# Index layer of a two-block transformer on one core: new column order, top-k rounds beside later columns, memory products between attention steps

## The reference

```python
def even_mixer(x, w_in, ckv_gain, w_uk, w_uv, sinks, w_out, rel_table):
    q_a, c_kv, q_i, k_i, w_i, q_b, k_b, v_b = split_cols(x @ w_in, EVEN_WIDTHS)   # 512,128,512,64,8,512,128,128
    o_a = dsa_attention(...)      # index scores pick 64 keys per query, attention over latents
    o_b = banded_attention(...)   # causal window of 128 keys, sinks
    return concatenate([o_a, o_b]) @ w_out

# in dsa_attention, per block of 128 queries
    act = relu(einsum('bqhd,bsd->bqhs', qi_b, k_i) * IDX_DIM ** -0.5)
    score = einsum('bqh,bqhs->bqs', wi_b, act)
    score = where(kpos <= qpos, score, -1e30);  sel = top_k(score, 64)

# in cross_attention
    k = mem @ w_k;  v = mem @ w_v
```

## Time and profile before

| | us |
|---|---|
| Median of 3 runs | 2604.91 (2604.16 to 2604.93) |
| Profiled execution | 2608.45 |
| Its span | 2606.7 |
| PE busy | 2524.2 (97%) |
| DVE, ACT, POOL busy | 1991.7, 1163.7, 74.9 |
| The changed stretch, 990.95 to 1126.70 | 135.75 |

### The profile page before, as it was taken

One profiled execution on the slowest core, in us unless ns is written; L12 is line 12 of the kernel. 1 busy time (PEld: TensorE's weight loads), 2 busy tenths in 40 slices (PEclk: granted clock), 3 DMA queues, 4 the chain that ended last, 5 costly groups with the idle time before them and its releaser, 6 DMA issues.

```text
span 2606.7 us, 42896 instructions
## 1 busy us (share of the span) xinstructions
PE 2524.2 (97%) x16960; PEld 2157.3 (83%) x16960; DVE 1991.7 (76%) x2450; ACT 1163.7 (45%) x1487; POOL 74.9 (3%) x104
## 2 busy tenths in 40 slices
PE   8999999999999999889999989999999999999998
PEld 5877888888879999678999787888888888888886
DVE  4958777778647885647888747888888888889887
ACT  4354100003311002442003646777777777777776
POOL 0100100000000000000001100000000000000000
PEclk9999999999999999999999999999999999999999
DMA  8714544443225544123554222999899989999996
GB/s 343 286 74 162 186 169 169 168 168 123 81 101 220 185 177 146 65 98 114 181 189 153 109 98 109 374 362 374 336 375 362 375 336 371 368 352 358 363 374 247
DMA packets 90393, 599.66 MB, mean 230 GB/s; under 512 B 9728, under 2 KB 12800, under 8 KB 23552
## 3 DMA queue, kind: packets, MB, share of 16 engines
q1 hardware_dynamic: 77280, 543.20, 55.2%
q0 software_dynamic: 12960, 54.26, 5.8%
HBM read 596.37 MB, written 1.05 MB: 229 GB/s over the span
## 4 chain that ended last, share of the span: by engine, by line
PE 91%; DVE 4%; ACT 2%; DMA 1%; issue 1%; SPq 0%; DVEq 0%; ACTq 0%
PE bank L1108 13%; PE bank L1111 13%; PE bank L1112 13%; PE bank L2275 8%; PE bank L2279 8%; PE bank L2278 8%; PE bank L2306 4%; PE bank L2310 4%; PE bank L2309 4%; PE bank L503 3%; DMA ring<-in_stream 1%; PE bank L1376 1%; ACT arena L1398 1%; PE bank L519 1%; PE bank L1355 1%; PE bank L543 1%
## 5 line engine op out<-in xcount | busy, mean ns | idle before, releaser
L928 DVE TENSOR_TENSOR ring_part<-ring,arena_part 128x2048 fp32r<-128x2048 f32 (+1 forms) x480 | 1077.8, 2275 | 28.5 <-ACT arena_part L2598 12.4
L2598 ACT ACTIVATE arena_part<-ring 128x2048 fp32r<-128x2048 f32 x339 | 647.5, 1920 | 196.4 <-DMA ring<-in_stream 195.3
L1108 PE MATMUL bank<-arena_part 128*128 128x256 f32 (+1 forms) x2184 | 699.5, 320 | 19.4 <-DVE h_part L928 6.4
L1112 PE MATMUL bank<-arena_part,ring_part 128*128 128x256 f32 (+1 forms) x2184 | 695.0, 318 | 0.0
L1111 PE MATMUL bank<-h_part,arena_part 128*128 128x256 f32 (+1 forms) x1656 | 526.4, 318 | 0.0
L1108 PEld LDWEIGHTS bank<-arena_part 128*128 128x128 f32 x2184 | 418.5, 192 | 57.5 <-issue 25.0
L1112 PEld LDWEIGHTS bank<-arena_part,ring_part 128*128 128x128 f32 x2184 | 418.6, 192 | 27.5
L2275 PE MATMUL bank<-arena_part,h_part 128*128 128x512 f32 x896 | 354.1, 395 | 0.0
L2279 PE MATMUL bank<-arena_part,h_part 128*128 128x512 f32 x896 | 349.6, 390 | 0.0
L2278 PE MATMUL bank<-ring_part,h_part 128*128 128x512 f32 x896 | 348.9, 389 | 0.0
L1111 PEld LDWEIGHTS bank<-h_part,arena_part 128*128 128x128 f32 x1656 | 317.3, 192 | 20.1
(11 more groups left out here) (350 smaller groups left out, 2867.6 us busy)
## 6 DMA issues: line engine op xcount, KB each, us to landing
ring<-in_stream SPq DMA_DIRECT2D x515, 1024.0 KB, 4.9
arena<-in_ada_stream POOLq DMA_DIRECT2D x80, 512.0 KB, 4.5
consts<-in_small POOLq DMA_DIRECT2D x1, 2800.0 KB, 11.5
arena<-in_c_rows POOLq DMA_DIRECT2D x2, 1024.0 KB, 6.1
arena<-in_ab_bias POOLq DMA_DIRECT2D x1, 2048.0 KB, 9.9
arena<-in_t_bias POOLq DMA_DIRECT2D x1, 2048.0 KB, 9.2
x_stream<-in_x_t SPq DMA_DIRECT2D x1, 1024.0 KB, 7.4
x_stream<-in_ctx_t SPq DMA_DIRECT2D x1, 1024.0 KB, 9.2
```

Source lines behind the costliest of these rows:

```text
L928: return nc.vector.tensor_tensor(low, value, high.bitcast(F32), ALU.subtract)
L1108: m = nc.tensor.matmul(out_ap, w_high, high, start=start, stop=False)
L1112: return nc.tensor.matmul(out_ap, w_low, high, start=False, stop=stop)
L2598: nc.scalar.activation(high, ring[:, where], ACT.Copy).then_inc(sem("moe_high"), 1)
```

## The change

The columns now come in the order q_i, k_i, c, q_a, q_b, k_b, v_b. PE makes six columns, the head weights and the sum of c's squares, and then lays index scores between the four q_a columns: four heads behind each. The slots are split by other engines: ACT rounds slots 2 to 7 and the first two of the output projection (`ev_rounded`, `slot_high_act`), DVE makes the low part of slot 2, POOL those of all others (`pool_low`), in one queue with the two masks. Three areas in turn hold the high parts. On DVE each add of a head of the second block of queries is followed by a top-k round of the first block; k_b and v_b are copied out behind the last round. The memory products are cut into pieces of four (`mem_group`) and put in front of certain steps of the two attentions on PE, in a bank of their own (7); the attention outputs share bank 6. ACT copies a group out at the steps of `DSA_DONE` and `BAND_DONE`. The latents and their squares move to another place. On the host, the columns of the weights are reordered.

```diff
-        ev_slot_high = next_slot_high(1, 8)
+        EV_AT = FFN_AT[1] + SLOTS_FFN
+        ev_areas = [part_area(8192, SLOT)] + [slot_high[(EV_AT + i) % 2] for i in range(2)]
+        ev_slot_high = {EV_AT + n: ev_areas[n % 3] for n in range(8)}
         OD_AT = FFN_AT[2] + SLOTS_FFN
...
+        cT = area(17616, 256)
         q_iT = area(1280, 1024, "p (c t) -> p c t", c=4)
...
+        EV_ATT_OUT, MEM_BANK = 6, 7
+        DSA_UNITS = {("T", a): (a // 2, 4) for a in range(6)}
+        DSA_DONE = {("S", 4): 0, ("V", 2): 1, ("V", 4): 2}
+        BAND_UNITS = {("T", 0): (4, 4), ("T", 1): (4, 4), ("V", 0): (5, 4), ("T", 2): (5, 4)}
+        BAND_DONE = {("V", 0): 4, ("V", 2): 5}
...
-            split_products(bk, w, 15, next_high, h_part, SEQ, ev_slot_high)
...
+            marks["ev_split"] = bk.count["slot_split"]
...
+            def ev_columns(n):
+                more_split_products(bk, w, n, next_high, h_part, SEQ, ev_slot_high)
+
+            def index_scores(t, heads):
+                for h in heads:
+                    b = bk.next_bank()
+                    pe.wait_ge(free(b), bk.emptied())
+                    r, c = half(h % 2), h // 2
+                    nc.tensor.matmul(PS[b][:, X2], q_iT[r, c, t * P:(t + 1) * P], k_iT[r, :], start=True, stop=True)\
+                        .then_inc(full(b), 1)
+
+            split_products(bk, w, 4, next_high, h_part, SEQ, ev_slot_high)
+            ev_columns(2)
+            index_taken = bk.all_freed(bk.turn - 6, 5)
             small_token_products("w_idx", 8)
             sum_pe(bk, "c_squared", lambda c: c_sq, SEQ, 1)
+            lat_from = []
+
+            def latent_query():
+                ev_columns(1)
+                lat_from.append(bk.freed(bk.turn - 1))
+
+            latent_query()
+            for taken in index_taken:
+                pe.wait_ge(*taken)
+            index_scores(0, range(4))
             rstd_pe(bk, SEQ)
-            pe.wait_ge(*bk.freed(bk.turn - 1))
+            c_normed = bk.freed(bk.turn - 1)
+            latent_query()
+            index_scores(0, range(4, 8))
+            pe.wait_ge(*c_normed)
             b = bk.next_bank()
             pe.wait_ge(free(b), bk.emptied())
             for t in range(2):
                 m = nc.tensor.transpose(PS[b][:, t * P:(t + 1) * P], cT[:, t * P:(t + 1) * P], ident)
             m.then_inc(full(b), 1)
+            c_tok_taken = bk.freed(bk.turn - 1)
+            for at in (0, 4):
+                latent_query()
+                index_scores(1, range(at, at + 4))
+            ev_columns(4)
+            band_from = [bk.freed(bk.turn - n) for n in (4, 3, 2, 1)]
+            ev_columns(1)
+            b = bk.next_bank()
+            pe.wait_ge(free(b), bk.emptied())
+            tiles = [w.tiles()[0] for _ in range(DC)]
+            for t in range(2):
+                for k in range(DC):
+                    m = nc.tensor.matmul(PS[b][:, t * P:(t + 1) * P], xv[:, k, t * P:(t + 1) * P], tiles[k],
+                                         start=k == 0, stop=k == DC - 1)
+            m.then_inc(full(b), 1)
+            band_from += [bk.freed(bk.turn - n) for n in (2, 1)]
             uk = small_at("w_uk", "p (c n) -> p c n", c=4)
-            for taken in bk.all_freed(bk.turn - 19, 16):
+            for taken in lat_from:
...
-            for taken in bk.all_freed(bk.turn - 24, 8):
+            for taken in bk.all_freed(bk.turn - 8, 8) + [c_tok_taken]:
                 pe.wait_ge(*taken)
-            mem_products()
+            mem_parts, mem_done = [], []
+
+            def mem_group(group, n):
+                begun = mem_done.count(group)
+                if begun == 0:
+                    pe.wait_ge(free(bk.fill(MEM_BANK)), bk.emptied())
+                    if group == 4:
+                        mem_parts.extend(w.slots(2))
+                for k in range(begun, begun + n):
+                    mem_done.append(group)
+                    if group < 4:
+                        tile, first = w.tiles()
+                        m = nc.tensor.matmul(PS[MEM_BANK][:, X2], tile, xv[:, k, SEQ:TT], start=k == 0, stop=k == DC - 1)
+                    else:
+                        t, half_at = group - 4, k // 4
+                        part = mem_parts[half_at][:, k % 4 * 512:(k % 4 + 1) * 512]
+                        m = nc.tensor.matmul(PS[MEM_BANK][:, :], xv[:, k, SEQ + t * P:SEQ + (t + 1) * P], part,
+                                             start=k == 0, stop=k == DC - 1)
+                        first = k % 4 == 0 and t == half_at
+                    if first:
+                        m.then_inc(sem("slots_used"), 1)
+                if begun + n == DC:
+                    m.then_inc(full(MEM_BANK), 1)
+
+            def mem_beside(units):
+                def beside(what, a):
+                    if (what, a) in units:
+                        mem_group(*units[what, a])
+                return beside
+
             pe.wait_ge(sem("bias_landed"), 48)
-            outs = attention_pe(bk, dsa_steps())
+            outs = attention_pe(bk, dsa_steps(), mem_beside(DSA_UNITS))
+            mem_group(3, DC)
...
+            for taken in band_from:
+                pe.wait_ge(*taken)
+            attention_pe(bk, band_steps(), mem_beside(BAND_UNITS))
 
...
+            def ev_rounded(n, begun=None):
+                slot_high_act(bk, EV_AT + n, ev_slot_high, fresh=begun is None, used=None if begun is None else EV_AT + begun + 1)
+
+            def index_relu(t, heads):
+                for h in heads:
+                    n = 8 * t + h
+                    if n >= 2:
+                        act.wait_ge(sem("score_added"), n - 1)
+                    to(relu_buf[n % 2], ACT.Relu, cols=SEQ, scale=64 ** -0.5)
+
+            ev_rounded(2)
             for c in range(4):
                 to(q_iT[:, c, :], cols=SEQ)
+                if c == 1:
+                    ev_rounded(3, begun=1)
+            ev_rounded(4, begun=2)
+            bk.turn += 2
+            sqrt_table()
+            act.wait_ge(*bk.freed(bk.turn - 1))
+            nc.scalar.activation(c_sq, cT, ACT.Square).then_inc(sem("c_squared"), 1)
             bk.turn += 1
+            root_act(bk, SEQ, 1, n=P)
+            to(q_aT[:, 0, :], cols=SEQ)
+            ev_rounded(5, begun=3)
+            index_relu(0, range(4))
+            bk.turn += 1
+            to(q_aT[:, 1, :], cols=SEQ)
+            index_relu(0, range(4, 8))
+            to(c_tok[:, :, :].rearrange("p t e -> p (t e)"), cols=SEQ)
+            for c in (2, 3):
+                to(q_aT[:, c, :], cols=SEQ)
+                if c == 2:
+                    ev_rounded(6, begun=4)
+                index_relu(1, range(4 * c - 8, 4 * c - 4))
             for c in range(4):
                 to(q_bT[:, c, :], cols=SEQ, scale=64 ** -0.5)
...
+                if c == 0:
+                    ev_rounded(7, begun=5)
...
+            slot_high_act(bk, EV_OUT, ev_out_high, fresh=True)
+
+            def mem_out(group):
+                b = bk.fill(MEM_BANK)
+                act.wait_ge(full(b), bk.filled())
+                if group < 4:
+                    ins = nc.scalar.activation(mem_keys[0][:, group, :], PS[b][:, X2], ACT.Copy)
+                else:
...
+            attention_act(bk, dsa_steps(), mem_beside(DSA_DONE))
+            mem_out(3)
...
+            slot_high_act(bk, EV_OUT + 1, ev_out_high, fresh=True)
+            attention_act(bk, band_steps(), mem_beside(BAND_DONE))
...
-            def split_ev(n, cols=SLOT):
-                at = FFN_AT[1] + SLOTS_FFN + n
-                split_slot(bk, at, None, used=at if n > 2 else None, highs=ev_slot_high, cols=cols)
+            slot_low_dve(bk, EV_AT + 2, ev_slot_high)
+            marks["ev_rounded"] = bk.count["slot_rounded"]
+            bk.up("slot_rounded", 7)
...
+            def add_index(t, h):
+                dve.wait_ge(*bk.freed(bk.turn))
+                bk.turn += 1
+                wi, s = w_heads[:, t, h:h + 1], idx_score[:, t, :]
+                rb = relu_buf[h % 2]
+                if h == 0:
+                    ins = nc.vector.tensor_scalar(s, rb, wi, None, ALU.mult)
+                else:
+                    ins = nc.vector.scalar_tensor_tensor(s, rb, wi, s, ALU.mult, ALU.add)
+                ins.then_inc(sem("score_added"), 1)
+                dve.wait_ge(sem("score_added"), bk.up("score_added"))
+
+            def top_round(t, r):
+                if r == 0:
+                    dve.wait_ge(sem("score_masked"), t + 1)
+                s, wk = idx_score[:, t, :], idx_work[:, t, :]
+                src = s if r == 0 else wk
+                nc.vector.max(top8[:, t, :], src).then_inc(sem("dve_step"), 1)
+                dve.wait_ge(sem("dve_step"), bk.up("dve_step"))
+                nc.vector.match_replace(wk, top8[:, t, :], src, -3e38).then_inc(sem("dve_step"), 1)
+                dve.wait_ge(sem("dve_step"), bk.up("dve_step"))
+
+            def top_mask(t):
```

(64 more changed lines are left out.)

121 lines of the change are left out of this document (27 added, 94 removed).

## The result

The changed kernel takes **2615.07 us** (median of 5 runs, 2613.68 to 2621.89) where the kernel before took 2604.93 beside it: a ratio of 1.0036, 95% interval 1.0026 to 1.0047. It is slower by 0.4%, outside the range of the prediction (2595 to 2612). In a second comparison, with 7 runs against 29 of before, the ratio was 1.0033 (1.0022 to 1.0044). That settles the size: some 9 us.

The account below looks back on a forecast made before the run. PE, busy 97% of the span, was taken as the bound. Columns and index lose 5.2 us, memory in the attention gains 9.6, net -4.4; DVE held by POOL adds 7.3, so +2.9 on 2604.9 gives 2607.8 us, range 2595 to 2612.

Parts of the forecast that it names:

- The wait for slot 6: Index layer's columns: PE waits for POOL's low part, queued behind its second mask; 8.4 us, 9.4 with DVE held.
- The exclusion: DVE work reading only SBUF is held while POOL forms a low part; 7.3 us in sum.
- the mask add: Second sparse step: DVE's add waits for output slot 0's low part on POOL, first turn 4.1 us later.
- the band's scaling: Band attention: DVE's first scaling waits for output slot 1's low part on POOL, 1.5 us.
- The 2.0 us of clock behind the sparse step's first turn: Sparse attention: PE's clock is low after the hole ahead of the first turn, 2.0 us.
- Rivals 1, 2 and 4: No exclusion for tensor-tensor forms (2600.5, 0.24); POOL's queue not late (2590.9, 0.14); memory groups delay PE's turns (2610.5, 0.08).
- The attention with memory in it and nothing held: Sparse scores to output projection, memory groups between turns: 62.2 us against the old 71.8, gain 9.6.
- later waits: Attention steps: waits after the held DVE instructions shrink by 1.3 us, as softmax and turns are then ahead.
- The charge of 2.0 us for the clock behind slot 6's wait: Index layer: PE's clock is low after the new stall, as after an earlier hole; 2.0 us charged.
- the account of part 1: Columns and index: some 6 us gained, less 8.4 stall, 2.0 clock and q_lat copies; 5.2 us lost.
- rival 3: Head-weight product: clock drops, dense columns follow at half clock, 2.4 us lost; 2610.2 or more, chance 0.12.
- a difference of spans carries over: Whole kernel: the span's change was added unchanged to the median time, 2604.9 + 2.9 us.

Follow-up runs that it names:

- low6_first: The changed kernel with POOL forming the low part of slot 6 ahead of the second mask instead of behind it; median 2608.1 us.
- adds_first: The changed kernel with all eight score adds of the second 128 tokens ahead of the first block's top-k rounds on DVE; median 2609.0 us.
- out_lows_dve: The changed kernel with the low parts of the first two output slots made by DVE behind the sparse step, not by POOL; index layer 133.50 us.
- adds_and_out_dve: The changed kernel with score adds ahead of top-k rounds and the first two output slots' low parts on DVE; median 2598.8 us, ratio 0.9975 to before.
- columns_alone: The changed kernel with memory products in one block ahead of the sparse attention again and two output banks in both attention steps; median 2620.1 us.
- memory_alone: The kernel before with only the change's memory groups between the turns of the two attention steps; median 2621.2 us.

## Why the prediction was wrong, point by point

**The steps that held.** The wait for slot 6 was forecast at 8.4 us, or 9.4 with the exclusion, because POOL's second mask comes about 1037: it was 8.7 us, and the mask came at 1039.49. The exclusion between DVE and POOL was taken from one scalar instruction on 16 columns and spread to all DVE work in SBUF: it held for tensor-tensor forms too, in the mask add (3.84 over its own 0.42, forecast 4.1), the band's scaling (2.24, forecast 1.5) and, in low6_first, an add (3.72). The max and replace rounds weren't held (0.43 and 0.41 us in adds_first beside the low part at 1032.23, as elsewhere), and they were covered, as forecast. The 2.0 us of clock behind the sparse step's first turn was 2.0. The sparse scores were forecast 70.1 us behind the first column (1060.1 + 1.0, from 990.95) and came after 70.7 in the first profile. From there to the output projection 68 to 70 us were forecast and 68.8 to 69.1 measured. Rivals 1, 2 and 4 are out.

**The sizes that were off inside it.** The attention with memory in it and nothing held was walked to 62.2 us; in out_lows_dve and adds_and_out_dve, which also have ACT's rounding off the chain, it took 60.7. The 1.1 us of half clock in that walk never came there: the two rows of out_lows_dve have clock 1.00. The 0.6 us between its sum of 62.8 and the 62.2 stands in no run. So the memory products between the turns are worth up to 71.8 - 60.7 = 11.1 us, not 9.6. Against that, the band's hold and the rounding cost 2.3 us together, where the sum had 1.5 and took 1.3 off for later waits. These nearly cancel.

**Readings that were wrong and did no harm.** The charge of 2.0 us for the clock behind slot 6's wait was 1.9, 2.2 and 2.4 in the three profiles, but the reading under it was wrong. Ahead of 978.07 there was no hole of 12 us in before:

```profile
978.07 0.36 PE L1108 MATMUL bank<-arena_part 128*128 128x256 f32 x1 [1.75 <-DVE ring_part L928]
```

It was 1.75 us, and the clock was at half speed for 3.4 us behind it (5 x 0.34 / 0.5), not for nearly 5; that the charge came out is luck. And the account of part 1 (6 gained, less 8.4 and 2.0 and 2.9 of copies) gives -7.3 us, not the -5.2 of the walk; the forecast used the walk.

**The step that failed** is rival 3's chance and its size: "the clock drops in the head-weight product", 0.12, 2.4 us. The sum put this term at nothing. The trace of before had shown the clock at 0.50 from 1042 on the earlier trace rows, behind the same piece of 8-column products. I read that as a drop *in* a stretch of small work, which dense columns around it would prevent. The dense columns didn't prevent it; they came to run at half speed. It happened in two of the three profiles of the change, at 1.7 and 3.4 us, and put the index layer at 141.4 and 143.3. With the 1.7 us that the same two lose at the output projection it is a mean of (1.95 + 3.77 + 2 x 1.7) / 3 = 3.0 us (0.3 of it the longer half speed behind slot 6), about half of what was missing. The chain was right, and the clock under it wasn't. Rival 3 had named the mechanism, at 2.4 us; its 2610.2 or more is still under the measured time.

A second step failed beside it: "a difference of spans carries over". It put the time outside the span at no change, and that grew by 1.4 us.

**The frame.** The forecast took 2604.9 as the base; the larger sample says 2606.5. That would have moved the forecast up to 2609.4, still some 6 us short of 2615.1 to 2615.8.

**The sum.** The mean index layer of the three profiles of after is 141.4 us, 5.7 over before. The rest of the span is 2471.0 in the mean of three against 2470.5 in two: +0.6, with the drop at the output projection in it. Outside the span (time less span) before spends 1.80 us, between 1.74 and 1.84 in all its runs; the change spends 2.1 to 3.6, 3.2 in the median: +1.4. Together 7.7. The median spans of all runs differ by a little more, 2612.6 - 2604.7 = 7.9, as the two profiled executions of before were 1.5 us over its median; 7.9 + 1.4 = 9.3 is the difference of the medians. Against the forecast's 2.9 that leaves 6.4 us: 2.8 in the index layer, 0.6 in the rest of the span, 1.4 outside it, and 1.6 that the profiles show less than the medians. Of the 2.8, the first profile, without a drop, has 0.8: 0.5 ahead of the sparse scores and 0.3 behind.

**What stays open.** What the 1.4 us outside the span are: columns_alone and memory_alone have 1.97 and 1.96, all others derived from the change 2.3 to 3.4 in the median, and no view shows that time. Why the clock also drops at the output projection in two of three profiles of the change. And where the profiled executions of before lost 1.5 us to its median.

## What to carry to other kernels

Read an engine's queue for what stands behind each wait: here a 0.4 us mask, put behind the eighth add, kept a weight slot from PE for 8.7 us, and moving only DVE's adds gave 6.8 us back. A low part on POOL is not free for DVE: place it where DVE works out of PSUM or not at all, and check whom a held instruction feeds, down to the bank that a copy behind it frees. And when a change moves a piece of small products from among other small work to between dense ones, price the clock behind it into the sum and take more than one profile: an execution with no drop looked like a forecast come true.

## What the runs showed of the hardware that I had not expected

- The clock fell while PE had no idle time in the profile: behind 32 products of 8 columns (3.5 us) PE was 100% busy and its mean clock was 0.66 over 5 us, or 0.57 over 8 us, or 1.00, in three executions of one kernel. In two pieces of 16, with a column between, it stayed at 1.00 in both profiles.
- A copy of 128x4 within SBUF took 4.37 us beside POOL's low part (0.17 without), while a custom operation of 128x256 with one input in PSUM kept its 0.48 us.
- The clock can spread the executions of one kernel with the same waits: the three profiles of the change have the same 8.7 us wait, and index layers of 139.5 to 143.3 us; the two of before are both at 135.7.
